# Up tiles of two MLPs with the high weights against high and low activations in one 512-column product

## The chip, the cores and the metric

The kernel runs on one core of one Trainium2 chip. The metric is the device time of one execution in microseconds (us). Three runs of the kernel before gave 896.41, 896.54 and 896.57 us; the median is 896.54 us.

## What is computed

The reference is a small two-mixer block on 256 tokens of width 1024, all in float32. First comes a hybrid layer (attention and gated linear attention), then MLP "a", then an mLSTM mixer, then MLP "b", then a gated output stage. Both MLPs are the same function with a hidden width of 4096:

```python
def sq_relu_mlp(h, w1, w2):
    return jnp.square(jax.nn.relu(h @ w1)) @ w2
```

MLP a is followed by a product with a row of modulation values (`gt2`), which the kernel sums up on VectorE from weight tile `ada11` (`silu(c) @ w_ada`).

## The kernel before, in words

**Split products.** TensorE multiplies fp32r operands. To keep float32 accuracy each operand x is split into a high part (x rounded to fp32r, a ScalarE `Copy`, `hi_part`, L1354) and a low part (x minus the high part, a VectorE subtraction, `lo_part`, L1856), and each product is the sum of three: low by high, high by high and high by low. `product` (L769) issues the three matmuls, each with a weight load of its own.

**Weights.** They arrive in units of 512 KB in a ring of four `raw` buffers. SyncE issues the load of unit u as soon as unit u-4 was cut (L703). ScalarE and VectorE cut a unit into `w_hi` and `w_lo`; the last of the two increments `unit_cut`. `w_hi` and `w_lo` have two tile places, so a tile can only be cut when the tile before the previous one has been used.

**An MLP.** Each has eight up tiles u0 to u7 (512 hidden features each) and eight down tiles d0 to d7. The order on TensorE is u0, u1, d0, u2, d1, ..., u7, d6, d7, so that a down tile never follows straight on its own up tile (except the last, which follows d6). An up tile is two groups g of two 128-feature blocks b; for each block and each of the 8 chunks k of the width, three matmuls with the weights stationary and 256 token columns moving: 96 matmuls. A group fills one PSUM bank, `psum[4 + 2 * c + g]`, with c alternating from tile to tile, so four banks serve two tiles in flight. A down tile has the activations stationary and 512 columns of weights moving: 48 matmuls. Its four outputs stay in banks 0 to 3 through the whole MLP.

**The hidden values.** For each group ScalarE takes the relu of the bank into `hid_r` (L1657) and squares it into `act_hi` (L1662); VectorE squares `hid_r` into `hid_h` (L2295) and subtracts `act_hi` for `act_lo` (L1856). `hlo_done` counts this last step, and the down tile waits for it. In a step of the loop, ScalarE and VectorE cut the next up tile when an up tile is done (`cut_step(tag, True, ...)`, during the down tile), then do the hidden values of the tile just finished (`hidden`), then wait for the down tile and cut the next one.

**The end of MLP a.** After the loop VectorE sums up `ada11`: `ada` takes four units of the same ring, two multiply-adds each (L1882, L1886), and one short addition (L1897). Only then does it cut d7 and do the hidden values of tile 7. TensorE does d6, then `ada_fin` (L789, a float32 product that adds up `ada_sum` over the partitions into bank 4), then `last_down` for d7. The units of d7 follow those of `ada11` in the ring. MLP b has no such sum there.

Of the kernel before, what the change touches and what calls it, by code (L numbers as in the profile page):

```python
# [15 lines left out]
F32 = mybir.dt.float32  # L16
# [8 lines left out]
P = 128  # L25
# [360 lines left out]
SCALED_LATER = ("n3", "n4", "n5")  # L386
AWAKE = {}
UP0 = {"a": 0, "b": 2 * FF_STEPS}
N_FIRST, N_SMALL, N_PARAMS = 2, 3, 6
GATE_K = 6 * RANK + 2  # L390
SMALL_HI = {"lr": 2, "gate_w": 4, "gate_x": 6, "p": 7}
# [3 lines left out]
def build(nc, a, out):  # L395
    with ExitStack() as ctx:
        def sb(name, shape, dt=F32):
            return ctx.enter_context(nc.sbuf_tensor(name, shape, dt))

        def sem(name):  # L400
            return ctx.enter_context(nc.semaphore(name))
# [2 lines left out]
        raw = sb("raw", [P, RAW, 2, NC])  # L404
        w_hi = sb("w_hi", [P, 2, 8, NC], F32R)
        w_lo = sb("w_lo", [P, 2, 8, NC], F32R)
        act_hi = sb("act_hi", [P, KC, 2 * T], F32R)
        act_lo = sb("act_lo", [P, KC, 2 * T], F32R)
        small_hi = sb("small_hi", [P, 512], F32R)
        small_lo = sb("small_lo", [P, 768], F32R)  # L410
        pick = sb("pick", [P, 16])
# [18 lines left out]
        silu_c = sb("silu_c", [P, KC, 2])  # L430
        silu_e = sb("silu_e", [P, KC, 2])
        silu_m = small[:, 0:256].rearrange("p (k v) -> p k v", k=KC)
        psum = [ctx.enter_context(nc.psum_tensor(f"bank{i}", [P, NC], F32)) for i in range(8)]

        ident, u_strict, l_strict, u_incl, l_incl, ones = (consts[:, i, :] for i in range(6))
        tri_pair = consts[:, 3:5, :]
# [121 lines left out]
        def head_of(name, h):  # L558
# [46 lines left out]
            sem(n) for n in ("head_sq", "head_ready", "head_turned", "head_y", "head_hi", "head_lo"))  # L605
        y_ready, y_turned, y_hi, y_lo = sem("y_ready"), sem("y_turned"), sem("y_hi"), sem("y_lo")
        res_ready = sem("res_ready")
        hid_done, relu_done, hsq_done, hhi_done, hlo_done = (
            sem(n) for n in ("hid_done", "relu_done", "hsq_done", "hhi_done", "hlo_done"))
        down_done, acc_done = sem("down_done"), sem("acc_done")  # L610
        gt_done, gt_ready = sem("gt_done"), sem("gt_ready")
        mr_ready, me_ready = sem("mr_ready"), sem("me_ready")
# [31 lines left out]

        def wait_landed(eng, round_, slot):
            eng.wait_ge(raw_in[slot], 16 * round_ + 16)

        def wait_used(eng, n):

# [111 lines left out]
        def _(pe):  # L761
# [21 lines left out]
            def acts(k):  # L783
                return (act_hi[:, k], act_lo[:, k])
# [94 lines left out]
            def turn(name, quarters=range(4)):  # L879

                i = TURN_AT[name]
                source = res if name in SCALED_LATER else x_norm2 if name == "n2" else x_norm
                if name == "n3" and quarters[0] == 0:
                    pe.wait_ge(relu_done, UP0["b"])
# [230 lines left out]
            def up(tag, i, c):  # L1115


                first = UNIT_AT[tag + "u1"] - 8
                ts = SPLIT_AT[tag + "u1"] % 2
                for g in range(2):  # L1120
                    if not (isinstance(i, int) and i < 2):
                        pe.wait_ge(relu_done, 2 * i + (UP0[tag] + g - 3))
                    for b in range(2):
                        col = (2 * g + b) * P
                        for k in range(KC):
                            if g == 0 and b == 0 and k % 2 == 0:
                                wait_cut(pe, 8 * i + (first + k // 2))
                            last = product(psum[4 + 2 * c + g][:, b * T:(b + 1) * T],
                                           (w_hi[:, ts, k], w_lo[:, ts, k]), acts(k), slice(0, T),
                                           slice(col, col + P), k == 0, k == KC - 1, feature_major=True)  # L1130
                    last.then_inc(hid_done, 1)

            def down(tag, i, c, first=False):
# [30 lines left out]
            def mlp(tag, name):  # L1164
                first_up(tag, name)
                up(tag, 1, 1)
                down(tag, 0, 0, first=True)
                with pe.Fori(0, FF_STEPS // 2 - 1) as k:
                    up(tag, 2 * k + 2, 0)
                    down(tag, 2 * k + 1, 1)  # L1170
                    up(tag, 2 * k + 3, 1)
                    down(tag, 2 * k + 2, 0)
                if tag == "a":
                    ada_fin(psum[4], 11).then_inc(gt_done, 1)

            def m_gates(part):
# [163 lines left out]
        def _(act):  # L1340
# [309 lines left out]
            def hidden(tag, i, c):  # L1650

                k = "ab".index(tag)
                for g in range(2):
                    act.wait_ge(hid_done, 2 * i + (UP0[tag] + g + 1))
                    if not (isinstance(i, int) and i == 0 and tag == "a"):
                        act.wait_ge(hsq_done, 2 * i + (UP0[tag] + g - 1))
                    act.activation(hid_r[:, g], psum[4 + 2 * c + g][:, :], ACT.Relu).then_inc(relu_done, 1)  # L1657
                for g in range(2):
                    act.wait_ge(relu_done, 2 * i + (UP0[tag] + g + 1))
                    if g == 0 and not (isinstance(i, int) and i < 2):  # L1660
                        act.wait_ge(down_done, i + ((FF_STEPS - 1) * k - 1))
                    act.activation(act_hi[:, 4 * c + 2 * g:4 * c + 2 * g + 2, T:2 * T],  # L1662
                                   hid_r[:, g].rearrange("p (b t) -> p b t", b=2), ACT.Square).then_inc(hhi_done, 1)

            def mlp(tag, name):
                if tag == "b":
                    for j in (2, 3):
                        split_unit("bu0", j)
                    turn(name, (2, 3))
                square_sum(name, res)  # L1670
                guess(name, TT)
                if name not in SCALED_LATER:
                    for g in range(2):
                        evac("pw", g)
                    turn(name)
                    for g in range(2, 4):
                        evac("pw", g)
                    evac("ada10", 0)
                split(tag + "u1")
                hidden(tag, 0, 0)  # L1680
                split(tag + "d0")
                with act.Fori(0, FF_STEPS // 2 - 1) as k:
                    for c in range(2):
                        cut_step(tag, True, 2 * k + c)
                        hidden(tag, 2 * k + (c + 1), (c + 1) % 2)
                        cut_step(tag, False, 2 * k + c)
                split(tag + "d7")
                if tag == "b":
                    exp_ln_set()
                hidden(tag, FF_STEPS - 1, 1)  # L1690
                if tag == "a":
                    act.wait_ge(gt_done, 1)
# [153 lines left out]
        def _(dve):  # L1846
# [437 lines left out]
            def cut_step(tag, up_, i):  # L2284
                n = tag + ("u2" if up_ else "d1")
                for j in range(4):
# [2 lines left out]
                    lo_part(w_lo[:, SPLIT_AT[n] % 2, s], raw[:, UNIT[n, j] % RAW],  # L2289
                            w_hi[:, SPLIT_AT[n] % 2, s]).then_inc(unit_cut, 1)  # L2290

            def hidden(tag, i, c):
                for g in range(2):
                    dve.wait_ge(relu_done, 2 * i + (UP0[tag] + g + 1))
                    dve.tensor_tensor(hid_h[:, g], hid_r[:, g], hid_r[:, g], ALU.mult).then_inc(hsq_done, 1)  # L2295
                for g in range(2):
                    dve.wait_ge(hsq_done, 2 * i + (UP0[tag] + g + 1))
                    dve.wait_ge(hhi_done, 2 * i + (UP0[tag] + g + 1))
# [4 lines left out]
            def mlp(tag, name):  # L2303
# [16 lines left out]
                split(tag + "d0")  # L2320
                with dve.Fori(0, FF_STEPS // 2 - 1) as k:
                    for c in range(2):
                        cut_step(tag, True, 2 * k + c)
                        hidden(tag, 2 * k + (c + 1), (c + 1) % 2)
                        cut_step(tag, False, 2 * k + c)
                if tag == "a":
                    for j in range(4):
                        ada(11, j)
# [347 lines left out]
```

## Time and profile before

| | |
|---|---|
| median of three runs | 896.54 us (896.41 to 896.57) |
| span of the profiled execution | 894.1 us |
| median less this span | 2.4 us |
| TensorE busy | 873.3 us, 98% of the span, 5520 matmuls |
| VectorE, ScalarE busy | 619.0 us (69%), 492.4 us (55%) |
| HBM traffic | 180 GB/s over the span |
| mean granted TensorE clock | 0.998 |

The span runs from the first instruction to the last; what the metric adds to it lies around the instructions. No other time of the profiled execution is given, so a change of the span is set against the median as it is. Matmuls are pipelined: the duration of one (0.28 us for 256 columns) is longer than the distance from its start to the next one's, and it is the distance between starts that sets the pace. Line numbers are those of the kernel before.

### The profile page before, as it was taken

How to read it: one execution, taken by the hardware profiler on the slowest of the kernel's cores; microseconds unless marked ns; L12 is line 12 of the kernel's file. 1: busy time of each engine (PE TensorE's matmuls, PEld its weight loads, DVE VectorE, ACT ScalarE, POOL GpSimd, SP SyncE). 2: the span in 40 equal slices, each digit the busy share in tenths (PEclk: the TensorE clock that was granted, in tenths of full speed). 3: DMA queues.
4: the chain of work that ended last, by engine and by line, in shares of the span. 5: the costliest groups of instructions: out<-in, count | busy, mean ns of one | idle time of the engine just before them, and what ended most of it. 6: DMA issues, size and time to landing. Idle time of an engine off the chain costs nothing.

```text
span 894.1 us, 14961 instructions
## 1 busy us (share of the span) xinstructions
PE 873.3 (98%) x5520; PEld 745.7 (83%) x5520; DVE 619.0 (69%) x986; ACT 492.4 (55%) x802; POOL 13.1 (1%) x26
## 2 busy tenths in 40 slices
PE   5999999999999999999999999999999999999996
PEld 2877777887888888899999998998888999999985
DVE  3579868889779978775555557766787755555575
ACT  4587766665565665574444444453755544444554
POOL 0110000000000000000000000000000000000001
PEclk9999999999999999999999999999999999999999
DMA  9954323345457776736555557354434865555531
GB/s 363 366 147 137 119 71 109 127 133 174 130 154 254 254 276 239 235 98 209 188 188 187 187 185 265 113 185 143 148 118 141 274 225 199 183 188 188 188 107 48
DMA packets 45266, 161.91 MB, mean 181 GB/s; under 512 B 5500, under 2 KB 5660, under 8 KB 45216
## 3 DMA queue, kind: packets, MB, share of 16 engines
q1 hardware_dynamic: 43200, 156.78, 52.2%
q0 software_dynamic: 1296, 3.78, 1.5%
q8 instruction: 35, 0.57, 0.3%
q10 hardware_dynamic: 720, 0.65, 0.2%
q14 instruction: 15, 0.12, 0.0%
HBM read 160.15 MB, written 1.05 MB: 180 GB/s over the span
## 4 chain that ended last, share of the span: by engine, by line
PE 87%; DVE 7%; ACT 3%; issue 2%; DMA 1%; SPq 0%; POOL 0%; POOLq 0%; DVEq 0%; ACTq 0%
PE bank L769 74%; DVE w_lo L1856 2%; PE bank L957 1%; PE bank L947 1%; PE bank L1250 1%; DMA arena<-in_early 1%; PE bank L1048 1%; PE bank L1070 1%; PE bank L1065 1%; ACT w_hi L1354 1%; PE bank L1272 1%; PE bank L905 1%; PE bank L964 1%; PE bank L978 1%; DVE act_lo L1856 1%
## 5 line engine op out<-in xcount | busy, mean ns | idle before, releaser
L1856 DVE TENSOR_TENSOR w_lo<-raw,w_hi 128x1024 fp32r<-128x1024 f32 x244 | 288.5, 1219 | 150.8 <-ACT w_hi L1354 150.2
L1354 ACT ACTIVATE w_hi<-raw 128x1024 fp32r<-128x1024 f32 x244 | 245.6, 1050 | 190.9 <-PE bank L769 159.8
L769 PE MATMUL bank<-w_hi,act_lo 128*128 128x512 f32 (+1 forms) x728 | 293.5, 403 | 0.3 <-DVE w_lo L1856 0.2
L769 PE MATMUL bank<-w_lo,act_hi 128*128 128x512 f32 (+1 forms) x728 | 282.7, 388 | 0.0
L769 PE MATMUL bank<-w_hi,act_hi 128*128 128x512 f32 (+1 forms) x728 | 282.3, 388 | 0.0
L769 PE MATMUL bank<-act_lo,w_hi 128*128 128x256 f32 x640 | 182.9, 286 | 1.9 <-DVE act_lo L1856 1.4
L769 PE MATMUL bank<-act_hi,w_hi 128*128 128x256 f32 x640 | 181.0, 283 | 0.0
L769 PE MATMUL bank<-act_hi,w_lo 128*128 128x256 f32 x640 | 181.0, 283 | 0.0
L769 PEld LDWEIGHTS bank<-w_lo,act_hi 128*128 128x128 f32 x728 | 136.7, 188 | 29.1
L769 PEld LDWEIGHTS bank<-w_hi,act_lo 128*128 128x128 f32 x728 | 136.9, 188 | 28.2 <-issue 1.4
L769 PEld LDWEIGHTS bank<-w_hi,act_hi 128*128 128x128 f32 x728 | 137.1, 188 | 25.7 <-issue 1.2
L769 PEld LDWEIGHTS bank<-act_lo,w_hi 128*128 128x128 f32 x640 | 122.6, 192 | 5.5 <-DVE act_lo L1856 3.4
L769 PEld LDWEIGHTS bank<-act_hi,w_hi 128*128 128x128 f32 x640 | 122.7, 192 | 0.5
L769 PEld LDWEIGHTS bank<-act_hi,w_lo 128*128 128x128 f32 x640 | 122.6, 192 | 0.0
L1856 DVE TENSOR_TENSOR act_lo<-arena,act_hi 128x512 fp32r<-128x512 f32 x64 | 41.6, 686 | 4.8 <-ACT act_hi L1354 4.1
L1886 DVE SCALAR_TENSOR_TENSOR small<-raw,silu_c,small 128x512 f32<-128x512 f32 x56 | 42.0, 750 | 4.2 <-DMA raw<-in_stream 2.4
L1354 ACT ACTIVATE act_hi<-arena 128x512 fp32r<-128x512 f32 (+1 forms) x33 | 20.0, 629 | 31.0 <-DVE arena L1983 25.1
L1425 ACT ACTIVATE arena<-bank 128x512 f32<-128x512 f32 x42 | 24.7, 592 | 16.5 <-PE bank L769 16.4
L1586 ACT ACTIVATE arena<-arena 128x256 f32<-128x256 f32 x64 | 24.1, 427 | 14.2 <-DVE arena L2239 11.8
L2246 DVE TENSOR_TENSOR arena<-arena 128x512 f32<-128x512 f32 x32 | 22.0, 687 | 12.2 <-ACT arena L1586 12.1
L957 PEld LDWEIGHTS bank<-arena 128*128 128x128 f32 x128 | 16.7, 191 | 7.2 <-issue 5.7
L2295 DVE TENSOR_TENSOR arena<-arena 128x512 f32<-128x512 f32 x32 | 20.7, 685 | 2.4 <-ACT arena L1657 2.2
(268 smaller groups left out, 729.7 us busy)
## 6 DMA issues: line engine op xcount, KB each, us to landing
raw<-in_stream SPq DMA_DIRECT2D x278, 512.0 KB, 4.4
arena<-in_early SPq DMA_DIRECT2D x16, 512.0 KB, 10.8
res<-in_x SPq DMA_DIRECT2D x2, 512.0 KB, 4.4
arena<-in_ctx SPq DMA_DIRECT2D x2, 512.0 KB, 11.1
res<-in_x POOLq DMA_DIRECT2D x1, 1024.0 KB, 8.6
arena<-in_norm_final POOLq DMA_DIRECT2D x1, 512.0 KB, 4.5
arena<-in_ple_b POOLq DMA_DIRECT2D x1, 512.0 KB, 5.1
out<-arena ACTq DMA_DIRECT2D x2, 256.0 KB, 2.7
```

The costliest lines, as they stand in the source:

```text
L769: last = pe.matmul(o, left, right, start=start and m == 0, stop=stop and m == 2, skip_group_check=shared)
L905: last = pe.transpose(psum[4 + b][:, k * P:(k + 1) * P], source[:, t, c:c + P], ident)
L947: pe.matmul(psum[4 + i % 2][:, :], q_t[:, h, t * P:(t + 1) * P], k_t[:, h // (QH // KVH), :], start=True, stop=True).then_inc(score_done, 1)
L957: last = pe.matmul(psum[7][:, t * P:(t + 1) * P], kv[:, c, c0:c0 + HD], prob_t[:, c, :], start=(c == 0), stop=(c == 3))
L964: last = pe.transpose(psum[6][:, c * P:(c + 1) * P], prob[:, j % 3, c * P:(c + 1) * P], ident)
L1354: return act.activation(o, i, ACT.Copy)
L1425: act.activation(o, i, ACT.Copy, scale=scale).then_inc(evac_act, 1)
L1586: ins = act.activation(gx_z[k % 3][:, m].rearrange("p (n h t) -> p n h t", h=2, t=LEVELS[k % N_LVL]), crossed(gx_d[k % 2], m, LEVELS[k % N ...
L1856: return dve.tensor_tensor(o, x, hi.bitcast(F32), ALU.subtract)
L1886: ins = dve.scalar_tensor_tensor(out=ada_sum, in0=w, scalar=c, in1=ada_sum, op0=ALU.mult, op1=ALU.add)
L2246: dve.tensor_tensor(gx_z[k % 3], gx_z[k % 3], keys_queries(h), ALU.mult).then_inc(lv_z, 1)
L2295: dve.tensor_tensor(hid_h[:, g], hid_r[:, g], hid_r[:, g], ALU.mult).then_inc(hsq_done, 1)
```

## The change

It concerns up tiles 1 to 7 of both MLPs (the second to the eighth); u0 keeps its three products (`first_up`).

1. `act_hi` and `act_lo` become the two halves of one tensor `act`, and the eight PSUM banks become one tensor `banks`. For each block and chunk two matmuls replace three: `w_lo` against 256 columns of `act_hi`, and `w_hi` against 512 columns, those of `act_hi` and those of `act_lo`, as one access pattern of two runs.
2. A block of 128 features now fills a bank of its own: columns 0 to 255 hold low by high plus high by high, columns 256 to 511 hold high by low. A tile takes all four banks 4 to 7, so TensorE waits for the sums of the tile before (`hid_sum`) where it waited for the relu of the tile two before.
3. ScalarE copies the second halves of a group's two banks to `hid_r` (`halves`) in place of the relu, and VectorE adds the first halves to it (`add_halves`, new). VectorE's square becomes a `scalar_tensor_tensor` max(x, 0) * x. ScalarE's square is replaced by a copy of `hid_h` to `act_hi`, which waits for VectorE.
4. In the orders of both engines `halves` and `add_halves` of a tile stand ahead of the cutting of the next up tile; those of tile 7 stand ahead of all that follows the loop, on VectorE the sum of `ada11`.
5. TensorE waits for all sums of MLP a ahead of `ada_fin`, and ahead of the first turn of `n3`.

```diff
+        def up_banks(g):
+            return banks[:, 6 - 2 * g:8 - 2 * g]
...
                 for g in range(2):
                     if not (isinstance(i, int) and i < 2):
-                        pe.wait_ge(relu_done, 2 * i + (UP0[tag] + g - 3))
+                        pe.wait_ge(hid_sum, 2 * i + (SUM0[tag] + g - 3))
+                    elif g == 1:
+                        pe.wait_ge(relu_done, 2 * "ab".index(tag) + 2)
...
-                            last = product(psum[4 + 2 * c + g][:, b * T:(b + 1) * T],
-                                           (w_hi[:, ts, k], w_lo[:, ts, k]), acts(k), slice(0, T),
-                                           slice(col, col + P), k == 0, k == KC - 1, feature_major=True)
+                            pe.matmul(o[:, 0:T], w_lo[:, ts, k, col], act_hi[:, k, 0:T], start=(k == 0), stop=False,
+                                      skip_group_check=True)
+                            last = pe.matmul(o.rearrange("p (v t) -> p v t", v=2), w_hi[:, ts, k, col], act[:, :, k, 0:T],
+                                             start=False, stop=(k == KC - 1), skip_group_check=True)
...
                 if tag == "a":
+                    pe.wait_ge(hid_sum, SUM0["b"])
                     ada_fin(psum[4], 11).then_inc(gt_done, 1)
...
+            def halves(tag, i):
+                for g in range(2):
+                    act.wait_ge(hid_done, 2 * i + (UP0[tag] + g + 1))
+                    act.wait_ge(hsq_done, 2 * i + (UP0[tag] + g - 1))
+                    act.activation(hid_r[:, g].rearrange("p (b t) -> p b t", b=2), up_banks(g)[:, :, T:2 * T],
+                                   ACT.Copy).then_inc(hid_half, 1)
...
                     for c in range(2):
+                        halves(tag, 2 * k + (c + 1))
                         cut_step(tag, True, 2 * k + c)
                         hidden(tag, 2 * k + (c + 1), (c + 1) % 2)
                         cut_step(tag, False, 2 * k + c)
+                halves(tag, FF_STEPS - 1)
                 split(tag + "d7")
...
+            def add_halves(tag, i):
+                for g in range(2):
+                    dve.wait_ge(hid_half, 2 * i + (SUM0[tag] + g - 1))
+                    x = hid_r[:, g].rearrange("p (b t) -> p b t", b=2)
+                    dve.tensor_tensor(x, up_banks(g)[:, :, 0:T], x, ALU.add).then_inc(hid_sum, 1)
...
-                    dve.tensor_tensor(hid_h[:, g], hid_r[:, g], hid_r[:, g], ALU.mult).then_inc(hsq_done, 1)
+                    dve.scalar_tensor_tensor(out=hid_h[:, g], in0=hid_r[:, g], scalar=0.0, in1=hid_r[:, g], op0=ALU.max,
+                                             op1=ALU.mult).then_inc(hsq_done, 1)
...
                     for c in range(2):
+                        add_halves(tag, 2 * k + (c + 1))
                         cut_step(tag, True, 2 * k + c)
                         hidden(tag, 2 * k + (c + 1), (c + 1) % 2)
                         cut_step(tag, False, 2 * k + c)
+                add_halves(tag, FF_STEPS - 1)
                 if tag == "a":
                     for j in range(4):
                         ada(11, j)
```

## Rows read from the trace of the kernel before

**Rows 1.** The page: busy time (share of the span) and instructions by engine.

```profile
PE 873.3 (98%) x5520; PEld 745.7 (83%) x5520; DVE 619.0 (69%) x986; ACT 492.4 (55%) x802; POOL 13.1 (1%) x26
```

**Rows 2.** The chain in order of time, MLP a (start us, us, what).

```profile
385.22 168.73 PE bank L769 x1104
```

**Rows 3.** Busy time by engine in one step of MLP a's loop.

```profile
430.77:453.18 22.41, 22.41 (x146) 20.52 (x145) 11.67 (x12) 9.81 (x12) 0.00 (x0) 1.00 0.57 188
```

**Rows 4.** Timeline of TensorE: ends of a down tile and of the up tile behind it.

```profile
431.93 0.39 PE L769 MATMUL bank<-w_lo,act_hi 128*128 128x512 f32 x1
...
441.45 0.39 PE L769 MATMUL bank<-w_lo,act_hi 128*128 128x512 f32 x1
441.67 0.28 PE L769 MATMUL bank<-act_lo,w_hi 128*128 128x256 f32 x1
...
453.19 0.40 PE L769 MATMUL bank<-w_hi,act_lo 128*128 128x512 f32 x1
```

**Rows 5.** Timeline of ScalarE, then VectorE, in the same step.

```profile
434.87 1.07 ACT L1657 ACTIVATE arena<-bank 128x512 f32<-128x512 f32 x2
...
453.48 3.91 ACT L1354 ACTIVATE w_hi<-raw 128x1024 fp32r<-128x1024 f32 x4 [7.70 <-PE bank L769]
...
437.90 1.28 DVE L1856 TENSOR_TENSOR act_lo<-arena,act_hi 128x512 fp32r<-128x512 f32 x2
```

**Rows 6.** Timeline of VectorE at the end of MLP a.

```profile
537.49 0.48 DVE L1882 TENSOR_SCALAR small<-raw,silu_c 128x512 f32<-128x512 f32 x1 [0.22 <-DMA raw<-in_stream]
...
539.99 4.82 DVE L1886 SCALAR_TENSOR_TENSOR small<-raw,silu_c,small 128x512 f32<-128x512 f32 x6 [1.23 <-DMA raw<-in_stream]
...
551.59 1.28 DVE L2295 TENSOR_TENSOR arena<-arena 128x512 f32<-128x512 f32 x2
552.80 1.28 DVE L1856 TENSOR_TENSOR act_lo<-arena,act_hi 128x512 fp32r<-128x512 f32 x2
```

**Rows 7.** Timeline of ScalarE there.

```profile
549.36 1.06 ACT L1354 ACTIVATE w_hi<-raw 128x1024 fp32r<-128x1024 f32 x1 [0.83 <-DMA raw<-in_stream]
```

**Rows 8.** Timeline of SyncE's queue, and below each issue its time to landing.

```profile
534.04 0.33 SPq L703 DMA_DIRECT2D raw<-in_stream  x1
...
raw<-in_stream SPq DMA_DIRECT2D x1, 512.0 KB, 3.4
...
538.94 0.33 SPq L703 DMA_DIRECT2D raw<-in_stream  x1
...
raw<-in_stream SPq DMA_DIRECT2D x1, 512.0 KB, 4.8
...
544.99 0.33 SPq L703 DMA_DIRECT2D raw<-in_stream  x1
...
raw<-in_stream SPq DMA_DIRECT2D x1, 512.0 KB, 4.3
```

**Rows 9.** Timeline of TensorE: start of d6, and the second matmul of d7.

```profile
542.87 0.40 PE L769 MATMUL bank<-w_hi,act_lo 128*128 128x512 f32 x1
...
554.88 0.40 PE L769 MATMUL bank<-w_hi,act_hi 128*128 128x512 f32 x1
```

**Rows 10.** TensorE's last matmul; TensorE busy and granted clock (fourth value) behind it.

```profile
885.77 0.28 PE L769 MATMUL bank<-w_lo,act_hi 128*128 128x256 f32 x1
...
890.00:891.00 1.00, 0.00 (x0) 0.86 0.00 0
891.00:892.00 1.00, 0.00 (x0) 0.50 0.31 117
```

**Rows 11.** Timeline of TensorE at the start: one kind of matmul twice.

```profile
7.73 2.28 PE L1272 MATMUL bank<-arena,small 128*32 128x256 f32 x16 [7.73 <-DMA arena<-in_early]
...
14.14 0.64 PE L1272 MATMUL bank<-arena,small 128*32 128x256 f32 x8
```

**Rows 12.** Timeline at the end of MLP b: VectorE, then TensorE.

```profile
847.12 1.29 DVE L1856 TENSOR_TENSOR act_lo<-arena,act_hi 128x512 fp32r<-128x512 f32 x2
...
850.76 0.39 PE L769 MATMUL bank<-w_hi,act_lo 128*128 128x512 f32 x1
```

More of the change, by code:

```diff
@@ L388 @@
 UP0 = {"a": 0, "b": 2 * FF_STEPS}
+SUM0 = {"a": 0, "b": 2 * (FF_STEPS - 1)}
 N_FIRST, N_SMALL, N_PARAMS = 2, 3, 6
@@ L406, in build @@
         w_lo = sb("w_lo", [P, 2, 8, NC], F32R)
-        act_hi = sb("act_hi", [P, KC, 2 * T], F32R)
-        act_lo = sb("act_lo", [P, KC, 2 * T], F32R)
+        act = sb("act", [P, 2, KC, 2 * T], F32R)
+        act_hi, act_lo = act[:, 0], act[:, 1]
         small_hi = sb("small_hi", [P, 512], F32R)
@@ L432, in build @@
         silu_m = small[:, 0:256].rearrange("p (k v) -> p k v", k=KC)
-        psum = [ctx.enter_context(nc.psum_tensor(f"bank{i}", [P, NC], F32)) for i in range(8)]
+        banks = ctx.enter_context(nc.psum_tensor("bank", [P, 8, NC], F32))
+        psum = [banks[:, i, :] for i in range(8)]
         ident, u_strict, l_strict, u_incl, l_incl, ones = (consts[:, i, :] for i in range(6))
@@ L607, in build @@
         res_ready = sem("res_ready")
-        hid_done, relu_done, hsq_done, hhi_done, hlo_done = (
-            sem(n) for n in ("hid_done", "relu_done", "hsq_done", "hhi_done", "hlo_done"))
+        hid_done, relu_done, hid_half, hid_sum, hsq_done, hhi_done, hlo_done = (
+            sem(n) for n in ("hid_done", "relu_done", "hid_half", "hid_sum", "hsq_done", "hhi_done", "hlo_done"))
         down_done, acc_done = sem("down_done"), sem("acc_done")
@@ L883, in turn @@
                 if name == "n3" and quarters[0] == 0:
-                    pe.wait_ge(relu_done, UP0["b"])
+                    pe.wait_ge(hid_sum, SUM0["b"])
                 for b in quarters:
@@ L1121, in up @@
                     if not (isinstance(i, int) and i < 2):
-                        pe.wait_ge(relu_done, 2 * i + (UP0[tag] + g - 3))
+                        pe.wait_ge(hid_sum, 2 * i + (SUM0[tag] + g - 3))
+                    elif g == 1:
+                        pe.wait_ge(relu_done, 2 * "ab".index(tag) + 2)
                     for b in range(2):
-                        col = (2 * g + b) * P
+                        col = slice((2 * g + b) * P, (2 * g + b + 1) * P)
+                        o = up_banks(g)[:, b]
                         for k in range(KC):
@@ L1173, in mlp @@
                 if tag == "a":
+                    pe.wait_ge(hid_sum, SUM0["b"])
                     ada_fin(psum[4], 11).then_inc(gt_done, 1)
@@ L1653, in hidden, with first_hidden @@
                 for g in range(2):
[L1654 to L1659, printed above, removed]
+                    act.wait_ge(hsq_done, 2 * i + (UP0[tag] + g + 1))
                     if g == 0 and not (isinstance(i, int) and i < 2):
                         act.wait_ge(down_done, i + ((FF_STEPS - 1) * k - 1))
-                    act.activation(act_hi[:, 4 * c + 2 * g:4 * c + 2 * g + 2, T:2 * T],
-                                   hid_r[:, g].rearrange("p (b t) -> p b t", b=2), ACT.Square).then_inc(hhi_done, 1)
+                    hi_part(act_hi[:, 4 * c + 2 * g:4 * c + 2 * g + 2, T:2 * T],
+                            hid_h[:, g].rearrange("p (b t) -> p b t", b=2)).then_inc(hhi_done, 1)
+            def first_hidden(tag):
+                for g in range(2):
+                    act.wait_ge(hid_done, UP0[tag] + g + 1)
+                    if tag == "b":
+                        act.wait_ge(hsq_done, UP0[tag] + g - 1)
+                    act.activation(hid_r[:, g], psum[4 + g], ACT.Relu).then_inc(relu_done, 1)
+            def halves(tag, i):
[4 more added lines that the diff above has]
+                                   ACT.Copy).then_inc(hid_half, 1)
             def mlp(tag, name):
@@ L1679, in mlp @@
                 split(tag + "u1")
+                first_hidden(tag)
                 hidden(tag, 0, 0)
@@ L2290, in cut_step @@
                             w_hi[:, SPLIT_AT[n] % 2, s]).then_inc(unit_cut, 1)
+            def add_halves(tag, i):
+                for g in range(2):
+                    dve.wait_ge(hid_half, 2 * i + (SUM0[tag] + g - 1))
+                    x = hid_r[:, g].rearrange("p (b t) -> p b t", b=2)
+                    dve.tensor_tensor(x, up_banks(g)[:, :, 0:T], x, ALU.add).then_inc(hid_sum, 1)
             def hidden(tag, i, c):
                 for g in range(2):
-                    dve.wait_ge(relu_done, 2 * i + (UP0[tag] + g + 1))
-                    dve.tensor_tensor(hid_h[:, g], hid_r[:, g], hid_r[:, g], ALU.mult).then_inc(hsq_done, 1)
+                    if isinstance(i, int) and i == 0:
+                        dve.wait_ge(relu_done, 2 * "ab".index(tag) + g + 1)
+                    else:
+                        dve.wait_ge(hid_sum, 2 * i + (SUM0[tag] + g - 1))
+                    dve.scalar_tensor_tensor(out=hid_h[:, g], in0=hid_r[:, g], scalar=0.0, in1=hid_r[:, g], op0=ALU.max,
+                                             op1=ALU.mult).then_inc(hsq_done, 1)
                 for g in range(2):
```

## The prediction

> **What bounds the kernel now.** I read the page first. TensorE is busy for 98% of the span [rows 1]. A full TensorE can still wait for others at the seams, so the next view is the chain in order of time. Through MLP a it is one unbroken piece of matmuls from 385.22 to 553.95 [rows 2]. One step of the loop (a down tile and an up tile) takes 22.41 us and TensorE is busy in all of it, while VectorE is busy 11.67 and ScalarE 9.81 us [rows 3]. So inside the loop only TensorE's pace counts. In the timeline its pace is plain: 96 matmuls of 256 columns from 441.67 to 453.19 are 0.120 us each, and 42 of 512 columns from 431.93 to 441.45 are 0.2267 us each [rows 4]. The granted clock is 1.00 there, the level of 2.4 GHz [rows 3]. 256 more columns cost 0.1067 us, which is exactly 256 columns at 2.4 GHz, and what is left of either distance is 0.0133 us per matmul, whatever its width. The other engines matter only where they are late for TensorE. The place to look is where their order changes and the cover is thin: the end of MLP a.
>
> **What the merge saves.** It leaves the number of columns as it is (256 + 512 for 3 times 256) and takes out one matmul and one weight load per block and chunk. If the fixed part of 0.0133 us goes with it, a tile saves 32 x 0.0133 = 0.427 us (11.52 to 11.09), and 14 tiles save 448 x 0.0133 = **5.97 us**. Bounds: the new moving operand has two runs, a form for which I have no row. If starting the second run costs as much as starting a matmul, nothing is saved; more than the whole fixed part can't be. I take the whole, since the fixed part is the same at both widths and so looks like the price of a matmul with its load. [...]
>
> **The loop itself stays covered.** Take 0 as the end of an up tile, the start of the down tile behind it. ScalarE starts 0.29 us later (453.19 to 453.48) [rows 4, 5]. It now first copies the second group's halves (two such reads of a bank take 1.07 together [rows 5]), then cuts 4 units (3.90) to 4.8. VectorE adds (0.69, like its square before) to 1.6 and finishes cutting at about 6.5. Then come two squares (0.75 and 0.66) to 7.9, ScalarE's copies behind them to 8.5, and the last subtraction to about 9.2. Before, it ended at 439.18, that is at 8.4 [rows 5]. The engines are wanted again when the down tile ends at 10.9, and the result one up tile later, at 22. So the extra addition, the wait of ScalarE's copy for VectorE and the 0.55 us by which the cutting starts later cost nothing here; if this cover were gone, they would cost 0.8 us a step. TensorE's new wait for `hid_sum` is met at 1.6, and the banks are wanted at 10.9. The first group's halves fall into ScalarE's and VectorE's idle time in the up tile. The weight loads start up to 0.6 us later and have 4.3 us to land where some 9 are open. At the end of MLP b the same chain counts to 9.2 plus a table load on ScalarE; before it ended at 848.41 for a down tile that begins at 850.7 [rows 12], so about 1.5 us are left. The first tile of each MLP keeps its relu, and the second group of u1 waits for it half a tile after it is done: nothing.
>
> **The end of MLP a is not covered.** Before, VectorE went from the loop straight to the sum of `ada11`, still during u7: it had cut the last unit at 544.81 [rows 6], 1.94 us into d6, which started at 542.87 [rows 9]. Now `add_halves` of tile 7 stands ahead of it and its second group can't begin until u7 is done. With 0 = 542.87:
> - ScalarE's copy 0.29 to 0.89; VectorE's addition to 1.62.
> - The first unit of `ada11` (0.48 and one multiply-add, which in a run of six takes 0.80 [rows 6]) to 2.9; the other three are 4.82 [rows 6], to 7.8. All four units have landed long before, they only hold the ring.
> - The ring now hangs on this: d7's fourth unit is issued when `ada11`'s fourth is cut, 0.18 later (544.81 to 544.99), so at 8.0, and takes 4.3 us to land [rows 8]. The landing behind a pause of the queue, at 534.04, was 3.4, one in a dense run, at 538.94, 4.8 [rows 8]; loads now come after a pause, at the same distance of 1.6 us. I take 4.1: 12.1.
> - ScalarE cuts at 12.2; VectorE is through with its half 2.23 after that start (549.36 to 551.59) [rows 6, 7]; two squares 1.41; copy of the second group 0.66; its subtraction 0.73: the hidden values are ready at 12.2 + 5.03 = 17.2. Before, 554.08 - 549.36 = 4.72 did for this, at 11.2.
> - TensorE finishes d6 and `ada_fin` as before: the matmul behind the first of d7 started at 554.88, so the first really began 0.23 earlier, at 554.65, or 11.8 [rows 9].
>
> **The stall is 17.2 - 11.8 = 5.4 us.** With landings of 3.4 and 4.8 it is 4.7 and 6.1. Who is late next: `mq`'s cutting moves from 12.5 to about 17.3, less than TensorE does, so nothing more is lost, and as TensorE has next to no idle time behind this point, nothing is given back.
>
> **Sum without the clock:** 896.54 - 5.97 + 5.4 = 896.0.
>
> **The clock.** A stall of 5.4 us is the only long pause of TensorE within the kernel. The trace has one such pause, at the end: the last matmul ends at 886.05, the mean granted clock is 0.86 from 890 to 891 and 0.50, the level of 1.2 GHz, behind that, so it fell at about 890.7, after some 4.7 us [rows 10]. The stall is longer than that. How long the low level lasts is seen at the start: eight matmuls of one kind took 1.14 us in the run that began at 7.73 and 0.64 us at 14.14 [rows 11], so up to 6 us after the start of work the rate was nearly half. If the low level holds for 2.6 to 6 us of work behind the stall, it costs half of that, 1.3 to 3.0 us; I take 2.0. **Sum with it: 898.0.** [...]
>
> **Rivals.**
> 1. The stall comes but the clock holds: 896.0. One pause of 4.7 us is thin evidence for another of 5.4, and where in the pause the clock falls may differ from run to run.
> 2. Faster: the stall is small. It decides at the landing of d7's units: if `ada11` were done under d6 with slack, only the 5.97 would be seen, 890.6; a stall under 4.2 us without a fall of the clock gives less than 894.75. The order on VectorE speaks against it.
> 3. The two-run operand costs as much as a start: no saving, 896.54 + 5.4 = 901.9, or 903.9 with the clock. For it: no row shows this form. Against: the columns are contiguous within each run, and the output is one run.
> 4. More is late at the seam than I count (TensorE at the low clock also delays what follows, a longer landing): 899 to 900.
>
> **How the numbers follow.** My forecast, the stall with a fall of the clock, has 0.37; its own range is 897.2 to 899.2. Rival 1 has 0.30 (895.3 to 896.8), rival 2 has 0.11, rival 3 has 0.12, rival 4 has 0.10. The range that holds 8 in 10 takes in the forecast, rivals 1 and 4 and the near edge of rival 2: 894.0 to 900.5. What a measurement of this kernel can tell from no change is 0.2%, or 1.8 us: faster is below 894.75, slower above 898.33. The forecast's own spread lies across the upper line, with about 0.15 of its 0.37 above it. Faster: 0.11. Slower: 0.15 + 0.12 + 0.10 = 0.37. Same: 0.22 + 0.30 = 0.52.
>
> **What the profile after would show.** In the loop the pair of matmuls takes 0.120 + 0.227 us and a step 21.98 us; TensorE stays without idle time. At the end of MLP a the first multiply-add of `ada11` starts behind u7, d7's units wait for their landing on ScalarE until 12 us into d6, and TensorE idles some 5 us ahead of d7, with VectorE's `act_lo` as the releaser. Behind that the granted clock shows 0.5 for some microseconds, or doesn't (rival 1). I would be wrong if the 512-column matmul with two runs takes more than 0.227 us, or if the sum of `ada11` is not what the seam waits for.

## Result: 901.45 us, and the profile after

Five runs of the changed kernel gave 901.02 to 902.89 us, median 901.45; five of the kernel before 896.41 to 897.70, median 896.57. The ratio is 1.0055, 95% interval 1.0044 to 1.0066: slower by 0.55%, some 4.9 us. The span of the profiled execution went from 894.1 to 899.2 us.

The page first. TensorE has 448 matmuls less and is busy for as long as before, and its share of the chain that ended last is down from 87% to 83%; VectorE is 20 us busier ([rows 1] for before).

```profile
span 899.2 us, 14112 instructions
PE 873.5 (97%) x5072; PEld 722.8 (80%) x5072; DVE 639.3 (71%) x1014; ACT 495.9 (55%) x802; POOL 13.1 (1%) x26
PE 83%; DVE 9%; ACT 3%; issue 2%; DMA 1%; SPq 0%; POOL 0%; POOLq 0%; DVEq 0%; ACTq 0%
```

Busy time in one step of MLP a's loop, from the start of a down tile to the next, against [rows 3]: TensorE is still never idle, VectorE has gone from 11.67 to 13.15 us, and the step is 22.24 us where it was 22.41.

```profile
430.88:453.12 22.24, 22.24 (x114) 18.81 (x113) 13.15 (x14) 10.13 (x12) 0.00 (x0) 1.00 0.54 190
```

The timeline of TensorE inside an up tile of that step, against [rows 4]. From 420.12 to 430.36 there are 29 pairs, 0.353 us each: on average the next matmul starts 0.117 us behind the one of 256 columns and 0.236 behind the one of 512. Three matmuls took 0.360 before. A pair at 0.347 had been forecast.

```profile
420.12 0.28 PE L1137 MATMUL bank<-act,w_lo 128*128 128x256 f32 x1
420.24 0.40 PE L1139 MATMUL bank<-act,w_hi 128*128 128x512 f32 x1
420.48 0.28 PE L1137 MATMUL bank<-act,w_lo 128*128 128x256 f32 x1
...
430.36 0.28 PE L1137 MATMUL bank<-act,w_lo 128*128 128x256 f32 x1
```

The end of MLP a, timeline of VectorE, then ScalarE, then TensorE ([rows 6, 7, 9] for before; start, duration, what, and in brackets the idle time and who ended it):

```profile
542.72 0.69 DVE L2322 TENSOR_TENSOR arena<-bank,arena 128x512 f32<-128x512 f32 x1 [4.97 <-ACT arena L1684]
543.33 0.48 DVE L1907 TENSOR_SCALAR small<-raw,silu_c 128x512 f32<-128x512 f32 x1
543.84 5.69 DVE L1911 SCALAR_TENSOR_TENSOR small<-raw,silu_c,small 128x512 f32<-128x512 f32 x7
...
557.91 1.29 DVE L1881 TENSOR_TENSOR act<-arena,act 128x512 fp32r<-128x512 f32 x2 [0.17 <-ACT act L1365]
```
```profile
554.23 1.06 ACT L1365 ACTIVATE w_hi<-raw 128x1024 fp32r<-128x1024 f32 x1 [0.57 <-DMA raw<-in_stream]
```
```profile
541.89 0.63 PE L775 MATMUL bank<-w_hi,act 128*128 128x512 f32 x2
...
552.83 1.02 PE L795 MATMUL bank<-small,consts 128*128 128x512 f32 x2
559.26 1.22 PE L775 MATMUL bank<-w_hi,act 128*128 128x512 f32 x2 [5.42 <-DVE act L1881]
560.28 0.63 PE L775 MATMUL bank<-w_lo,act 128*128 128x512 f32 x1
...
562.77 0.62 PE L775 MATMUL bank<-w_hi,act 128*128 128x512 f32 x2
```

VectorE idles for 4.97 us until ScalarE's copy of tile 7's second group, and only then starts the sum of `ada11`, at 543.33 in place of 537.49. ScalarE gets d7's last unit at 554.23, 12.3 us into d6, and the hidden values are ready at 559.20. TensorE has ended `ada_fin` at 553.70 (552.83 and some 0.87 us; in `e5` below the next matmul starts 0.86 us behind it) and stands until 559.26: 5.55 us. The granted clock (fourth value of the windows view, TensorE alone) fell in that pause:

```profile
557.00:558.00 1.00, 0.00 (x0) 1.00 0.95 315
558.00:559.00 1.00, 0.00 (x0) 0.88 0.79 299
559.00:560.00 1.00, 0.74 (x2) 0.50 0.67 262
560.00:561.00 1.00, 1.00 (x4) 0.50 0.18 74
561.00:562.00 1.00, 1.00 (x4) 0.50 0.00 0
562.00:563.00 1.00, 1.00 (x5) 0.91 0.74 197
```

It is at 0.50 from about 558.8 to 562.2. The nine matmuls from 559.26 to 562.77 took 3.51 us where nine at 0.2267 take 2.04: 1.47 us lost.

Where the 5.1 us of the span come from, read at the same instruction in both timelines:

| TensorE reaches | before | after | shift | gained in this part |
|---|---|---|---|---|
| first product of u0, MLP a | 385.22 | 385.56 | +0.34 | +0.34 |
| first product of d6 | 542.87 | 541.89 | -0.98 | -1.32 |
| first turn of `n3`, behind d7's first half | 562.85 | 568.92 | +6.07 | +7.05 |
| first product of d0, MLP b | 705.33 | 711.66 | +6.33 | +0.26 |
| last matmul | 885.77 | 890.95 | +5.18 | -1.15 |

Seven tiles of MLP a at 0.19 us are the 1.32. The seam is 5.55 + 1.47 = 7.02. In the fourth part u1 of MLP b saves its 0.19 too, so 0.45 us are lost there; TensorE eats through that tile's first chunks faster than they are cut. Its waits for `w_lo` at 701.25 and 702.38 and the slower starts just behind them cost some 0.64 us, where the kernel before lost 0.24 at one such wait. The 0.34 us at the start lie ahead of everything that the change touches.

### The profile page after: what moved, and what is told of

Its sections match the earlier page's. It is cut to its first block, busy times and chain, and to the rows that moved or that the text cites. A ratio compares the mean times of both kernels' runs of the same rounds, so it can differ in the third digit from the quotient of the medians.

```text
span 899.2 us, 14112 instructions
## 1 busy us (share of the span) xinstructions
PE 873.5 (97%) x5072; PEld 722.8 (80%) x5072; DVE 639.3 (71%) x1014; ACT 495.9 (55%) x802; POOL 13.1 (1%) x26
## 4 chain that ended last, share of the span: by engine, by line
PE 83%; DVE 9%; ACT 3%; issue 2%; DMA 1%; SPq 0%; POOL 0%; POOLq 0%; DVEq 0%; ACTq 0%
PE bank L775 53%; PE bank L1139 12%; PE bank L1137 6%; DVE w_lo L1881 3%; PE bank L963 1%; DVE small L1911 1%; PE bank L953 1%; DMA arena<-in_early 1%; PE bank L1261 1%; PE bank L1054 1%; ACT w_hi L1365 1%; PE bank L1076 1%; PE bank L1071 1%; ACT arena L1450 1%; DVE act L1881 1%
## 5 line engine op out<-in xcount | busy, mean ns | idle before, releaser
L775 PE MATMUL bank<-w_hi,act 128*128 128x512 f32 (+1 forms) x1456 | 457.8, 396 | 5.7 <-DVE act L1881 5.4
L775 PEld LDWEIGHTS bank<-w_hi,act 128*128 128x128 f32 x1456 | 266.8, 189 | 60.9 <-DVE act L1881 6.5
L775 PE MATMUL bank<-w_lo,act 128*128 128x512 f32 (+1 forms) x728 | 283.4, 389 | 0.0
L775 PEld LDWEIGHTS bank<-w_lo,act 128*128 128x128 f32 x728 | 137.0, 188 | 29.2
L1139 PE MATMUL bank<-act,w_hi 128*128 128x512 f32 x448 | 159.0, 399 | 0.0
L1137 PE MATMUL bank<-act,w_lo 128*128 128x256 f32 x448 | 126.0, 281 | 0.2 <-DVE w_lo L1881 0.2
L1139 PEld LDWEIGHTS bank<-act,w_hi 128*128 128x128 f32 x448 | 84.2, 188 | 20.7
L1137 PEld LDWEIGHTS bank<-act,w_lo 128*128 128x128 f32 x448 | 84.6, 189 | 1.2 <-DVE w_lo L1881 0.8
L775 PE MATMUL bank<-act,w_hi 128*128 128x256 f32 x384 | 71.7, 287 | 2.0 <-DVE act L1881 1.5
L775 PEld LDWEIGHTS bank<-act,w_hi 128*128 128x128 f32 x384 | 59.5, 191 | 5.3 <-DVE act L1881 3.7
L775 PE MATMUL bank<-act,w_lo 128*128 128x256 f32 x192 | 54.2, 282 | 0.0
L1881 DVE TENSOR_TENSOR act<-arena,act 128x512 fp32r<-128x512 f32 (+1 forms) x65 | 42.6, 688 | 9.0 <-ACT act L1365 8.3
L775 PEld LDWEIGHTS bank<-act,w_lo 128*128 128x128 f32 x192 | 36.7, 191 | 0.0
## 6 DMA issues: line engine op xcount, KB each, us to landing
arena<-in_early SPq DMA_DIRECT2D x16, 512.0 KB, 10.9
arena<-in_ctx SPq DMA_DIRECT2D x2, 512.0 KB, 10.9
```

The costliest lines, as they stand in the source:

```text
L775: last = pe.matmul(o, left, right, start=start and m == 0, stop=stop and m == 2, skip_group_check=shared)
L1137: pe.matmul(o[:, 0:T], w_lo[:, ts, k, col], act_hi[:, k, 0:T], start=(k == 0), stop=False, skip_group_check=True)
L1139: last = pe.matmul(o.rearrange("p (v t) -> p v t", v=2), w_hi[:, ts, k, col], act[:, :, k, 0:T], start=False, stop=(k == KC - 1), skip_gro ...
L1881: return dve.tensor_tensor(o, x, hi.bitcast(F32), ALU.subtract)
```

## Experiments

Two questions: is the seam made by the place of the sum alone, with the clock as a part of its price, and why does a pair take 0.353 us and not 0.347? Times of the kernel before on the same chips were 896.39 us (median of 15 runs) for `e1` to `e4`, 896.28 (of 17) for `e5` to `e8` and 896.39 (of 11) for `e9` to `e11`.

**e1, the sum ahead of the halves again.**

```diff
-                add_halves(tag, FF_STEPS - 1)
                 if tag == "a":
                     for j in range(4):
                         ada(11, j)
+                add_halves(tag, FF_STEPS - 1)
                 split(tag + "d7")
```

> On VectorE the sum of ada11 stands ahead of add_halves of tile 7 again; all else is the changed kernel. Theory (the seam is 7.0 us: 5.55 us of stall and 1.47 us at the low clock, both caused by that order): the stall falls to under 1 us, the clock stays at 1.00, and the time is 901.45 - 7.0 = 894.4 us, 2 us below the kernel before. Rival (the stall comes from the longer chain of the hidden values, not from the place of the sum): most of the stall stays and the time is over 899 us.

Measured: 894.34 us (11 runs, 893.67 to 895.51), ratio to before 0.9976 (0.9967 to 0.9985). In the timeline of TensorE the stall is gone:

```profile
552.70 1.02 PE L795 MATMUL bank<-small,consts 128*128 128x512 f32 x2
553.89 0.73 PE L775 MATMUL bank<-w_hi,act 128*128 128x512 f32 x2 [0.17 <-DVE act L1881]
554.46 0.40 PE L775 MATMUL bank<-w_lo,act 128*128 128x512 f32 x1
```

`ada_fin` ends at 553.57, and 0.3 us later d7 begins, at a granted clock of 1.00 from 553 on. One call moved behind the sum is worth 7.1 us and turns the change from 0.55% slower to 0.24% faster. The rival, that the longer chain of copy, addition, square, copy and subtraction makes the stall, falls: that chain is all there.

**e8, the late sum alone**, in the kernel before:

```diff
                 if tag == "a":
+                    dve.wait_ge(hid_done, 2 * FF_STEPS)
                     for j in range(4):
                         ada(11, j)
```

> The kernel before with one addition: VectorE waits for the end of u7 of MLP a ahead of the sum of ada11, so that it starts 0.3 us into d6, without any other part of the change. Theory (the place of the sum alone makes the seam): the sum starts at 543.2 in place of 537.5, TensorE stalls for 5.55 less the 1.2 us of copy and addition and 0.3 us of the longer chain, 4.0 us, and the time is 900.6 us with the clock at 1.00 and up to 902.1 us if it falls. Rival (the longer chain of the hidden values makes the stall): under 898 us.

Measured: 903.04 us (5 runs, 901.91 to 903.27), ratio 1.0066 (1.0053 to 1.0079), some 5.9 us. The stall is what had been forecast, 3.99 us, and the clock fell in it, 0.4 us before its end. Timeline and windows of TensorE:

```profile
555.43 1.02 PE L789 MATMUL bank<-small,consts 128*128 128x512 f32 x2
560.44 0.79 PE L769 MATMUL bank<-w_hi,act_lo 128*128 128x512 f32 x1 [3.99 <-DVE act_lo L1856]
561.03 0.63 PE L769 MATMUL bank<-w_hi,act_hi 128*128 128x512 f32 x1
```
```profile
558.00:560.00 2.00, 0.00 (x0) 1.00 0.86 268
560.00:562.00 2.00, 1.56 (x4) 0.51 0.78 301
562.00:564.00 2.00, 2.00 (x7) 0.64 0.70 184
```

The median lies 0.9 us above the upper end expected, and the seam isn't the reason. In the profiled execution, of 903.27 us, the clock had fallen once more, near the start, where the wait that was added does nothing yet (windows of TensorE):

```profile
16.00:20.00 4.00, 2.66 (x12) 0.67 1.03 411
```

Its MLP a begins at 386.86 where that of the kernel before began at 385.22, 1.6 us late. From there to the last matmul it takes 5.75 us more than the kernel before, which would put the time at 902.0. The two runs with the highest mean clocks took 901.91 and 901.97 us, the other three 903.04 to 903.27. One wait, with no matmul changed, costs more than the whole change gained or lost.

**e4 and e5, something for TensorE to do in the stall:** filler products of 512 columns in float32, 11 in `e4` (the diff) and 6 in `e5`.

```diff
                     ada_fin(psum[4], 11).then_inc(gt_done, 1)
+                    keep_awake(psum[7], 11)
```

> Eleven float32 matmuls of 512 columns into bank 7, whose result nobody reads, follow ada_fin on TensorE and fill the stall ahead of d7 (11 x 0.43 = 4.8 of 5.55 us). Theory (1.47 us of the seam are the low clock): the stall's place stays, the clock stays at 1.00, and the time is 900.0 us. Rival (the clock costs nothing, since what follows d7 waits for others anyway): 901.45 us. If the filler ends after the hidden values are ready it costs the excess, at most 0.5 us.

Measured: 904.14 us (4 runs), ratio 1.0085 (1.0069 to 1.01): a miss of my sizing. The eleven float32 products of 512 columns ran as 22 matmuls, 0.411 us each, and went on until 562.6, past the end of the stall.

```profile
553.60 9.61 PE L783 MATMUL bank<-consts 128*128 128x512 f32 x22
562.64 1.03 PE L775 MATMUL bank<-w_hi,act 128*128 128x512 f32 x2
```

> The filler of the fourth kernel again, sized by what it measured: its eleven float32 products ran as 22 matmuls of 0.411 us, 9.0 us in all, past the end of the stall. Six products are 4.9 us and end before the hidden values are ready. Theory (1.47 us of the seam are the low clock): no fall of the clock and 900.0 us. Rival (the low clock costs nothing): 901.45 us.

Measured: 899.97 us (5 runs, 899.05 to 901.01), ratio 1.0037 (1.0024 to 1.005). The pause ahead of d7 is 0.58 us and d7 runs at a granted clock of 1.00 from its first matmul (timeline of TensorE):

```profile
553.67 5.31 PE L783 MATMUL bank<-consts 128*128 128x512 f32 x12
559.57 0.73 PE L775 MATMUL bank<-w_hi,act 128*128 128x512 f32 x2 [0.58 <-DVE act L1882]
560.13 0.40 PE L775 MATMUL bank<-w_lo,act 128*128 128x512 f32 x1
```

So 1.5 us of the seam are the clock (901.45 less 899.97), and 5.55 the stall itself.

**e3, the merge alone undone.**

```diff
-                            last = pe.matmul(o.rearrange("p (v t) -> p v t", v=2), w_hi[:, ts, k, col], act[:, :, k, 0:T],
-                                             start=False, stop=(k == KC - 1), skip_group_check=True)
+                            pe.matmul(o[:, 0:T], w_hi[:, ts, k, col], act_hi[:, k, 0:T], start=False, stop=False,
+                                      skip_group_check=True)
+                            last = pe.matmul(o[:, T:2 * T], w_hi[:, ts, k, col], act_lo[:, k, 0:T],
+                                             start=False, stop=(k == KC - 1), skip_group_check=True)
```

> The 512-column product is undone: three matmuls of 256 columns per block and chunk again, with the new places of the sums, so only the matmul count differs from the changed kernel. Theory (merging itself is worth 96 x 0.120 - 32 x 0.3533 = 0.21 us per tile, 3.0 us over 14 tiles): 904.4 us. Rival (merging is worth nothing and the step of 22.24 us has another cause): 901.45 us.

Measured: 904.42 us (4 runs), ratio 1.0089 (1.0073 to 1.0104). By the medians the merge is worth 3.0 us. That is a little too much: in the profile of `e3` the clock was low (0.50) for 6.8 us at the seam, from 558.0 to 564.8, and not for 3.4. Ahead of d6 and behind the first turn of `n3` the two profiles differ by 1.33 and 1.29 us, so 2.6 us are the merge. The step is 22.42 us, from 419.82 to 531.92 in five steps, just that of the kernel before: the new addition, the copy that waits for the square and the banks shared by all tiles cost nothing in the loop.

**e2, one run in place of two.** The moving operand of the 512-column product is 512 neighbouring columns of `w_hi`, so the up tiles' values are others than the reference's.

```diff
-                            ... w_hi[:, ts, k, col], act[:, :, k, 0:T],
+                            ... w_hi[:, ts, k, col], w_hi[:, ts, k, :].rearrange("p (v t) -> p v t", v=2),
```

> The 512-column matmul of up tiles 1 to 7 takes one contiguous run of 512 columns of w_hi as its moving operand in place of the two runs of act; the up tiles' values are therefore not those of the reference. Measured in the changed kernel: a pair takes 0.3533 us where 0.3467 was predicted. Theory (the second run costs 6.7 ns): the pair takes 0.347 us, an up tile 11.09, and the time is 898.5 us. Rival (it is the alternation of a short and a long matmul, whatever is read): the pair stays at 0.353 us and the time at 901.45 us.

Measured: 901.8 us (4 runs), ratio 1.0059 (1.0044 to 1.0074), as the changed kernel, and the same gaps between starts (timeline of TensorE):

```profile
424.49 0.28 PE L1137 MATMUL bank<-act,w_lo 128*128 128x256 f32 x1
424.60 0.40 PE L1139 MATMUL bank<-w_hi 128*128 128x512 f32 x1
424.83 0.28 PE L1137 MATMUL bank<-act,w_lo 128*128 128x256 f32 x1
```

From 420.25 to 430.13 a pair takes 0.353 us here too, so the second run costs nothing that shows. My bound in the prediction was built on it, and it wasn't the cause of the missing 6 to 7 ns of a pair.

**e11, no change of width.** `w_lo` too takes all 512 columns, alternating as before; this adds the product of low and low.

```diff
-                            pe.matmul(o[:, 0:T], w_lo[:, ts, k, col], act_hi[:, k, 0:T], start=(k == 0), stop=False,
+                            pe.matmul(o.rearrange("p (v t) -> p v t", v=2), w_lo[:, ts, k, col], act[:, :, k, 0:T],
+                                      start=(k == 0), stop=False,
```

> Alternating as in the changed kernel, but w_lo too takes all 512 columns (the low by low product is added), so the width never changes. Theory (the extra 6.7 ns of a pair come from the change of width): a pair takes 2 x 0.2267 = 0.4533 us and a step 10.9 + 32 x 0.4533 = 25.4 us. Rival (a 512-column matmul with weights stationary costs 6.7 ns more in itself): a pair takes 0.467 us and a step 25.8 us.

Measured: 936.86 us (one run, on the order of `e1`), and by the profile a step of 25.39 us and evenly spaced starts (timeline of TensorE):

```profile
421.71 0.39 PE L1137 MATMUL bank<-act,w_lo 128*128 128x512 f32 x1
...
424.66 0.39 PE L1139 MATMUL bank<-act,w_hi 128*128 128x512 f32 x1
```

From 421.71 to 424.66 there are 13 gaps, 0.227 us each. A 512-column matmul with weights stationary, two runs and all, costs what it costs in a down tile, 0.2267 us [rows 4]. What is left as the cause of the extra is that the width changes from one matmul to the next.

**e7, e9 and e6, fewer changes of width.** On the order of `e1`, in each group of n input chunks the wait and the matmul of `w_lo` for each, then the matmul of `w_hi` for each, with n of 2, 4 and 8.

```diff
-                        for k in range(KC):
+                        for k0 in range(0, KC, n):
+                            for k in range(k0, k0 + n):
...
+                            for k in range(k0, k0 + n):
...
```

> As the kernel before it, but in groups of two: two matmuls of w_lo, then two of w_hi, so half of the changes of width are left. Theory: a pair takes 0.350 us, 14 x 0.107 = 1.5 us go: 892.8 us. Rival: 894.3 us.

> Groups of four matmuls of w_lo, then four of w_hi, in the order of the first kernel. Loop steps measured so far: 22.23 us alternating, 22.03 in groups of two, 22.05 in groups of eight; 21.98 would be the full saving. Theory (only strict alternation costs; any grouping takes most of it away): 22.02 to 22.06 us a step and 892.4 us. Rival (the cost falls with the number of width changes): a step between 21.98 and 22.01 us.

> On top of the order of the first kernel (894.34 us): within each 128-feature block the eight matmuls of w_lo (256 columns) come first, then the eight of w_hi (512 columns). Theory (the 6.7 ns by which a pair exceeds 0.3467 us are the price of changing width twice): one eighth of the changes is left, a pair takes 0.3475 us, a tile 11.12, and 14 x 0.187 = 2.6 us go: 891.7 us. Rival (each 512-column matmul with weights stationary costs 6.7 ns more, in whatever order): 894.3 us.

> Groups of two with the contiguous 512 columns of w_hi as moving operand (up tiles not those of the reference). Theory (two runs cost nothing): the step stays at 22.03 us. Rival (what is left over 21.98 us is the second run): 21.98 us.

| matmuls in a row | kernel | step of the loop, us | above 21.99 us | time, us | ratio (95%) |
|---|---|---|---|---|---|
| 1 | e1 | 22.23 | 0.24 | 894.34 | 0.9976 (0.9967 to 0.9985) |
| 2 | e7 | 22.03 | 0.04 | 892.38 | 0.995 (0.9937 to 0.9963) |
| 2, one run | e10 | 22.03 | 0.04 | 892.81 (one run) | |
| 4 | e9 | 22.13 | 0.14 | 893.38 | 0.9966 (0.9955 to 0.9978) |
| 8 | e6 | 22.05 | 0.06 | 896.13 | 0.9986 (0.9975 to 0.9997) |

21.99 us is 22.42 - 0.427, the full saving. The steps are read on ScalarE, whose first cut of a down tile starts with each step. For `e7` these are the first and the sixth of MLP a, so 110.13 us are five steps:

```profile
420.38 3.90 ACT L1368 ACTIVATE w_hi<-raw 128x1024 fp32r<-128x1024 f32 x4 [2.80 <-PE bank L775]
...
530.51 3.90 ACT L1368 ACTIVATE w_hi<-raw 128x1024 fp32r<-128x1024 f32 x4 [2.80 <-PE bank L775]
```

Grouping brings back most of what was missing, and `e7` at 892.38 us beats both kernels. `e10` shows once more that the second run adds nothing, 22.03 us a step with it and without. Of the steps that had been expected none came out to the hundredth: `e7` took 22.03 us (expected 10.9 + 32 x 0.350 = 22.10) and `e6` 22.05 (22.02), and `e9` with 22.13 missed both the theory (22.02 to 22.06) and its rival (21.98 to 22.01). Four in a row pay more than two, though they change half as often.

The starts of single matmuls show where the extra lies. Behind eight narrow matmuls (256 columns) the wide ones (512) of `e6` start about 0.235, 0.235, 0.229, 0.231 and 0.231 us apart, and then 0.227. So going from narrow to wide has a price, and it has died out five matmuls later. The kernel before pays it too, once a step, where a down tile follows an up tile. There the first five gaps of d6, from 542.87 [rows 9] to 544.03, take 1.16 us and the next five 1.13. In `e6` wide matmuls stand ahead of d6, and its first five take 1.13 at once (timelines of TensorE, before, then `e6`):

```profile
544.03 0.39 PE L769 MATMUL bank<-w_lo,act_hi 128*128 128x512 f32 x1
...
545.16 0.39 PE L769 MATMUL bank<-w_hi,act_hi 128*128 128x512 f32 x1
```
```profile
541.98 0.62 PE L775 MATMUL bank<-w_hi,act 128*128 128x512 f32 x2
...
543.11 0.39 PE L775 MATMUL bank<-w_lo,act 128*128 128x512 f32 x1
```

A shared bank isn't needed for it, since d6 writes other banks than the up tile ahead of it. Nor is the change of what is stationary the reason, since `e6` has that too and its d6 starts at full pace. At uniform paces a step would take 48 x 0.2267 + 32 x (0.120 + 0.2267) = 21.97 us, and with three narrow products 22.40. The kernel before, with one such change a step, takes 0.02 us more than that; `e6`, with four, 0.08; `e9`, with eight, 0.16. That is 0.020 us a change. Where only two or one wide matmul follow, a change costs less: 0.05 us for 16 (`e7`) and 0.26 for 32 (`e1`), 0.003 and 0.008 each.

`e6` has a better loop than `e9` and yet is 2.8 us slower. The spans of the two profiles differ by 3.4 us: 1.4 of them lie ahead of MLP a, behind a fall of the clock near the start as in `e8`, and 2.0 behind the first turn of `n3`. Timeline and windows of TensorE at the start of MLP b show how the second part begins:

```profile
694.88 0.51 PE L1138 MATMUL bank<-act,w_lo 128*128 128x256 f32 x2 [0.63 <-DVE w_lo L1884]
696.01 0.51 PE L1138 MATMUL bank<-act,w_lo 128*128 128x256 f32 x2 [0.63 <-DVE w_lo L1884]
```
```profile
694.00:696.00 2.00, 0.75 (x4) 1.00 0.86 281
696.00:698.00 2.00, 1.99 (x7) 0.67 0.87 328
698.00:700.00 2.00, 2.00 (x7) 0.50 0.97 348
```

In u1, whose weights are being cut as TensorE needs them, the first group now runs through all four units with only the short matmuls between, and waits 0.63 us for each of the last two. The clock fell behind this, though no single pause was longer than 0.64 us. Of its 12 runs eight are at 895.99 to 896.67 us and four at 892.70 to 894.23, the four with the highest mean clocks.

## Why the prediction was wrong

The time lies 0.95 us above the stated range and 3.4 us above the predicted 898.0.

- **"What the merge saves", 5.97 us, failed in its size.** The step on record is "I take the whole, since the fixed part is the same at both widths and so looks like the price of a matmul with its load". It saved 0.19 us a tile where 0.427 were forecast: 14 tiles are 2.7 us by the table of shifts, and undoing it in `e3` cost 3.0 us by the medians and 2.6 by the profiles. The missing 3.3 us are the gap to the result. The 2.4 GHz of the prediction is the rate of columns in the rows, 256 columns in 0.1067 us at a granted clock of 1.00; at 0.50, in `e8` from 561.03 to 563.17, five matmuls of 512 columns take 0.428 us each, 1.2 columns a ns. That the fixed part is the same at both widths was no finding: one line through two points gives that. That part was read in stretches of one width each; the new order alternates, and that has a price of its own of 6 to 7 ns a pair (`e11`, `e2`). The rows read before had a sign of it: the down tile begins at 430.77 [rows 3], its pace was taken from 431.93 on [rows 4], and the five gaps left out take 0.232 us each, not 0.2267. The sign of being wrong that was put on record, a wide matmul taking more than 0.227 us, was met with 0.236, but not by the two runs. The bounds below this term, 0 and 5.97, held it, but I weighted them as a yes or no (0.12 for no saving at all) and left nothing for half of it. The rival in which nothing is saved forecast 901.9 or 903.9; the time is near its first number by another route.
- **The seam was right in cause and size.** Forecast were a stall of 5.4 us behind `ada11`, with d7's last unit cut from 12.2 us into d6 and the hidden values ready at 17.2 us; measured 5.55, 12.3 and 17.3. `e1` and `e8` show the place of the sum as its cause, by taking it away and by making it alone.
- **The fall of the clock was right,** and its price of 2.0 us (1.3 to 3.0) was 1.47 by the profile and 1.5 by `e5`. No row of before shows the 2.6 us of work at which that range begins; measured were some 2.9 us, from 559.26 to 562.2.
- **The loop stayed covered,** as forecast: no idle time on TensorE, and `e3` gives the old step to 0.01 us. At the end of MLP b nothing was lost either.
- **"Nothing more is lost" was some 0.4 us short:** u1 of MLP b, where TensorE lives from hand to mouth on the cuts, was taken to be as well covered as a loop step.
- The forecast's direction, a result near no change, came from two large terms of opposite signs, and a mistake of 3 us in one of them was enough. The measured saving, 2.7, in my own sum would have given 901.3; that this is so near 901.45 is partly luck, since the clock cost 0.5 us less than its term and u1 of MLP b some 0.4 more.

What stays open: what in TensorE makes the wide matmuls behind a change slower, and why a change costs 0.020 us where four or eight of a width stand in a row and only 0.003 or 0.008 where it is two or one.

## What to carry to other kernels

When an operation is added to an engine's written order, look less at its own duration than at what it waits for and at what is queued behind it: a 0.69 us addition, covered everywhere in the loop, cost 7 us at the one place where it stood ahead of work that freed a buffer ring, and moving that work one place forward brought it all back. A pause of TensorE can cost more than its length: that of 5.55 us here cost another 1.5 at the low clock behind it. And a price per instruction read from uniform stretches need not hold for a mix (0.347 us a pair by them, 0.353 measured); look at the first instructions behind the place where one form gives way to another, bound the new mix in between and try groupings of the same instructions, which here were worth another 2 us.

## What the runs showed of the hardware

- **Changing widths.** In `e6`, behind matmuls of 256 columns, the first five gaps between matmuls of 512 are longer than 0.227 us, by 0.028 us together; the gap behind the first of 256 columns after 512 is shorter (0.113 for 0.120). 256 and 512 columns alternating take 0.353 us a pair, while uniform stretches give 0.120 + 0.227. Pairs in groups of two take (22.03 - 10.90) / 32 = 0.348. Whether the 512 columns come as one run or two made no difference: 0.353 us a pair in `e2` and in the changed kernel, 22.03 us a step in `e10` and in `e7`.
- **The clock fell in pauses of 4.1 to 5.7 us, and once behind shorter ones.** Counted from the end of `ada_fin`, it fell 3.0 us into a pause of 5.7 (`e3`), 3.7 us into one of 4.1 (`e8`) and 5.1 us into one of 5.6 (the changed kernel), and in `e6` behind some 2 us, with two pauses of 0.63, in which TensorE was busy for 0.75 us in pieces. It then stayed low (0.50) for about 3.4 us (6.8 in `e3`), the rest of the pause included.
- **In four of the thirteen profiles it also fell near the start.** TensorE works there with pauses (in `e7` 0.55 us for a load and 1.34 for `act`, both between 14 and 18 us); the kernel before has such pauses too, of 0.55 and 1.22 us, at 1.00. The windows view of `e7` has the fall:

```profile
16.00:20.00 4.00, 2.81 (x12) 0.63 1.03 410
20.00:24.00 4.00, 4.00 (x38) 0.94 1.04 412
```

  Runs of the kernel before lie in two groups, probably for this kind of reason, 895.4 to 896.8 and 897.5 to 897.9 us, the second with mean clocks of 0.995 to 0.996 and the first of 0.997 to 0.998. That only the fall near the start separates them was not tried. The profiles of `e6`, `e8` and `e10` have that fall too, and in these four MLP a begins at 386.5 to 386.9 us, against 384.7 to 385.6 in all others.
